# Convolution groups 1 to 3 of a two-layer hybrid block: weight columns stream past stationary tokens

## The chip, the cores and the metric

The kernel runs on one core of a Trainium2 chip. The metric is the device time of one execution in microseconds. Three executions before the change took 2537.07, 2537.81 and 2538.84 us; the median is 2537.81 us.

## The reference, cut to what matters

Two hybrid layers (a latent attention, pooling and convolution mixer), then a third block with attention and two wide feed-forward parts, on 256 tokens of width 2048. The change touches the convolution branch of both hybrid layers:

```python
D_CONV = 512; CONV_WIDTH = 3; DEPTH = 2

def conv_mixer(h, b_gate, c_gate, conv_w):
    u = c_gate * h
    y = lax.conv_general_dilated(u, conv_w[:, None, :], window_strides=(1,),
                                 padding=((CONV_WIDTH - 1, 0),), dimension_numbers=('NWC', 'WIO', 'NWC'),
                                 feature_group_count=D_CONV)
    return b_gate * y

def hybrid_layer(x, ...):
    proj = x @ w_in
    (q_lat, kv_lat, k_rope, g_mla, p_in, g_pool, c_h, c_b, c_c, g_conv) = jnp.split(proj, split_idx, axis=-1)
    y_mla = mla_mixer(...) * jax.nn.silu(g_mla)
    y_pool = pool_mixer(p_in, w_pool, pool_scale) * jax.nn.silu(g_pool)
    y_conv = conv_mixer(c_h, c_b, c_c, conv_w) * jax.nn.silu(g_conv)
    mix = jnp.concatenate([y_mla, y_pool, y_conv], axis=-1)
    out = mix @ w_out + b_out
    return layernorm(DEEPNORM_ALPHA * x + out, ln_g, ln_b)
```

## The kernel before, in words

All weights stream from HBM in slabs of up to 128 x 2048 numbers (1 MB), in one fixed order, written down by `plan()` as regions with so many slabs each. SyncE (SP) loads a slab into one of four `raw` buffers. ScalarE (ACT) rounds it to `high` (`split_high`, L1328), VectorE (DVE) makes `low = raw - high` (`split_low`, L1735), each in two halves of 1024 columns, into one of two buffers. The matrix engine (PE) multiplies high by high, high by low and low by high, so that fp32r matmuls give nearly fp32 results. Each engine's program goes through the same slots, one per slab (`walk`, L551). In a slot k, ACT makes the second half of slab k+1, then the steps of the slot, then the first half of slab k+2, then what it has to do with the finished products; DVE follows the same pattern. What else is done in a slot, attention heads among it, is given by the table `STEPS` (`layer_steps`, L224). Everything on an engine is in program order; other engines are waited for by semaphores.

There are two kinds of product. In a "tile" slab the weights are stationary: one slab is one tile of 128 output features by 256 tokens, and PE does 16 pairs, L923 with 512 moving columns (tokens high and low) and L927 with 256. In the regions `out`, `mem`, `heads`, `up` and `wide` the tokens are stationary and 512 weight columns stream past them: `product_natural` (L934) does three matmuls of 512 columns (L937 to L939) for each token block and each row of the slab, 24 per slab. The output then has tokens on the partitions.

Each hybrid layer has the regions `in_a`, `uq`, `uk`, `uv`, `in_b`, `in_c`, `pool`, `in_d`, `out`, `mem`. `in_d` has 13 tile slabs: the convolution's fourth tile of group 0, then four tiles (gate, h, c, b) for each of the groups 1 to 3. Six of the twelve are in `TURNED_OVER` (L342): eight L923 first and then eight L927, and so on. The other six alternate and have attention steps in their middle (`middle_of`, L941). For each tile, ACT copies the low half of the sum out of PSUM (L1382) and DVE adds the two halves (L1859, L1864). When a group is there, DVE multiplies h by c (L2087), applies the three taps (L2088 to L2091), multiplies by the silu of the gate (L2094) and by b (L1861) into `mix`. `mix` is split in four chunks of four tiles into `mixs`, high by ACT (L1684) and low by DVE (L2162). PE waits for chunk n of the order `MIX_ORDER` (L221; here 2, 0, 1, 3) at the start of slab n of `out` (L1164, semaphore `mix_l`). Chunk 3 is the convolution; its split was made between `in_d` and `out` (L1689, L2334).

The region `up` already turns token-major results back with DVE's 32 x 32 transposes (`hidden_turn`, L1778), and `wide` does so as well (L2007 to L2015). These are the forms that the change uses again.

Of the kernel before, what the change touches and what calls it, by code (L numbers as in the profile page):

```python
# [15 lines left out]
P = 128  # L16
# [64 lines left out]
def plan():  # L81
    regions = []
    for layer in range(DEPTH):
# [5 lines left out]
            Region(f"in_d{layer}", 13, (8, 8), 13, 2),  # L89
# [11 lines left out]
    s = t = g = pairs = lows = units = ups = wides = 0  # L101
    used = {}
    for r in regions:
# [6 lines left out]
        r.up, r.wide = r.name[:2] == "up", r.name[:4] == "wide"  # L110
# [4 lines left out]
        r.kind = next((k for n, k in (("up", "unit"), ("wide", "unit"), ("down", "down"), ("uq", "uq"), ("uk", "uk"), ("uv", "uv"),  # L115
# [5 lines left out]
        r.array = {"in_": "w_in", "uq": "w_uq", "uk": "w_uk", "uv": "w_uv", "pool": "w_pool", "out": "w_out",  # L121
# [3 lines left out]
                       next(n for n in ("in_", "uq", "uk", "uv", "pool", "out", "mem", "nat", "heads",  # L125
# [7 lines left out]
        r.span = 4 if r.up else WIDE  # L133
        r.unit0, r.up0, r.wide0 = units, ups, wides
        ups, wides = ups + r.up * r.n // r.span, wides + r.wide * r.n // r.span
        units = ups + wides
# [87 lines left out]
def layer_steps(layer):  # L224
    steps = {}

    def put(slot, *step):
        for name, first in (("in_a", 0), ("uq", 16), ("uk", 20), ("uv", 21), ("in_b", 23), ("in_c", 31),
                            ("pool", 33), ("in_d", 34), ("out", 48)):
# [31 lines left out]
    put(48 + 4, "shift", ln)  # L261
    put(48 + 5, "moments", ln, 0)
    put(48 + 8, "moments", ln, 1)
    put(48 + 12, "moments", ln, 2)
    for n in range(4):
        put(48 + 10 + n, "memory", 8 * layer + 2 * n, 8 * layer + 2 * n + 2)
# [94 lines left out]
def build(nc, t):  # L361

    with ExitStack() as ctx:
# [18 lines left out]
        memk = at("memk", [P, MEM, S], F32)  # L382
        memv = at("memv", [P, TB, MEM * P], F32)
# [50 lines left out]
        stage = at("stage", [P, TB, 2 * S], F32)  # L434
        scale_b = at("scale_b", [P, 2 * S], F32)
# [71 lines left out]
        unit_scaled = sem("unit_scaled")  # L507
        wide_out, wide_turned, wide_added, wide_squared, wide_folded = (
# [88 lines left out]
        def unit_bank(r, k, b):  # L597

            n = r.unit_in_part + k // r.span + int(r.name[-2])
# [226 lines left out]
        def acc_of(r, T):  # L826
# [3 lines left out]
            if r.name == "mixout" and T < r.t0 + 2 or after_norm(r) and r.t0 + 2 <= T < r.t0 + 4 \  # L830
                    or r.name == "down11" and T < r.t0 + 2:
                return flat(score[T % 2][:, :, :])
            return acc[T % 2][:, :]
# [12 lines left out]
        def gates_done(layer, tile):  # L846

            return 10 * layer + (tile // 4 + 1 if tile < 8 else tile - 5)
# [71 lines left out]
        def _(eng):  # L920
# [20 lines left out]
            def middle_of(r, k):  # L941
# [5 lines left out]
                if r.name[:4] == "in_d":  # L947
                    return (8, 9, 10, 11, 11 + 2 * r.layer, 12 + 2 * r.layer, 8)[k // 2]
                return 8

            def slot(r, k, i):
# [3 lines left out]
                halfway = [x for x in steps if r.kind in ("tile", "natural") and (  # L955
                    r.kind == "tile" and x[0] in ("turn", "mixv", "lat_sum") or x not in SCORES_FIRST and x[0] in ("memory_feature", "scores", "forget_turn", "cum", "decay")
# [11 lines left out]
                def bank_free(tile, per):  # L968
# [68 lines left out]
                elif r.kind == "unit":  # L1037
                    u, q_ = divmod(k, r.span)
                    if q_ == 0:
# [8 lines left out]
                    last_row = KT - 1 if r.up else CT - 1  # L1048
                    for piece in range(2):
                        piece_ready(piece)  # L1050
                        for b in range(TB):
                            for c in range(per):
                                row = 4 * q_ + per * piece + c
# [4 lines left out]
                                last = product_natural(unit_bank(r, k, b), (xs if r.up else hidden)[:, row, :],  # L1058
# [112 lines left out]
            def unit_bank_free(r, u, i):  # L1171
# [7 lines left out]
                else:  # L1179
                    eng.wait_ge(stored, val(r.t0 + 4 * (u - 1), 4, i))  # L1180

# [145 lines left out]
        def _(eng):  # L1327
# [13 lines left out]
            def slot(r, k, i):  # L1341
# [44 lines left out]
                if last_of_unit(r, k):  # L1386
                    (unit_gates if r.up else wide_copies)(r, k + 1 - r.span, i)
# [18 lines left out]
            def wide_copies(r, k, i):  # L1406
# [4 lines left out]
                for b in range(TB):  # L1411
# [4 lines left out]
                    eng.activation(wide_nat[:, b, :], unit_bank(r, k, b), ACT.Copy, scale=0.5).then_inc(wide_out, 1)  # L1416

# [313 lines left out]
        def _(eng):  # L1731
# [66 lines left out]
            def store(r, k, i, tile, per):  # L1798
# [19 lines left out]
                if r.name[:3] == "out":  # L1818
                    b, w = tile % TB, slice(512 * (tile // TB), 512 * (tile // TB + 1))
                    done(eng.tensor_tensor(z[:, b, w], acc[T % 2][:, :], x_tok[:, b, w], ALU.add))  # L1820
# [36 lines left out]
                elif r.name[:4] == "in_d" and tile % 4 == 0:  # L1857

                    done(eng.tensor_tensor(branch[:, 2, :], first, second, ALU.add), True)  # L1859
                    g = (tile + 3) // 4  # L1860
                    ins = eng.tensor_tensor(mix[:, 12 + g, :], mix[:, 12 + g, :], branch[:, 2, :], ALU.mult)  # L1861
                    final(ins, r.layer + 1 if g == GROUPS - 1 else None)
# [3 lines left out]
            def final(ins, count):  # L1866

                if count:
                    ins.then_inc(mix_final, 1)
                    eng.wait_ge(mix_final, count)  # L1870
                else:
                    step_(ins)
# [622 lines left out]
```

## Time and profile before

| what | value |
|---|---|
| median of three executions | 2537.81 us (2537.07 to 2538.84) |
| the profiled execution, its own time | 2537.32 us |
| its span, first to last instruction | 2535.5 us |
| PE busy | 2513.9 us, 99% |
| DVE busy | 1848.0 us, 73% |
| ACT busy | 1315.6 us, 52% |
| HBM read | 475.72 MB, 188 GB/s over the span |
| granted TensorE clock, mean | 1.000 |

PE's busy time is the union of its matmuls; they are pipelined, so the pitch from start to start says what one costs, not its duration. The DMA share is that of the core's 16 DMA engines. The chain of work that ended last lies on PE for 83% of the span.

### The profile page before, as it was taken

What the parts mean: (1) busy time and instruction counts of PE and PEld (TensorE: products, weight loads), DVE (VectorE), ACT (ScalarE), POOL (GpSimd) and SP (SyncE); (2) the same over time, 40 slices, a digit from 0 to 9 for tenths busy, and PEclk for the clock granted to TensorE, in tenths of its full rate; (3) what the DMA queues carried; (4) which work ended last, traced back from release to release, by engine and by line L of the source; (5) the groups of instructions that cost most, each with busy time, mean ns of one, the idle gap of its engine ahead of it and who ended that gap; (6) DMA issues with size and microseconds to landing.
All of it is one profiled execution on the core that took longest, in us unless ns stands there. A gap on an engine that the chain in (4) does not pass through costs nothing.

```text
span 2535.5 us, 33176 instructions
## 1 busy us (share of the span) xinstructions
PE 2513.9 (99%) x12124; PEld 2111.3 (83%) x12124; DVE 1848.0 (73%) x2980; ACT 1315.6 (52%) x1893; POOL 17.5 (1%) x20
## 2 busy tenths in 40 slices
PE   7999999999999999999999999999999999999999
PEld 6888888888888888888888887888888888888888
DVE  8777658777658777677777785678777767777766
ACT  6665565565566444444444454775544444444443
POOL 2000000000000000000000000000000000000000
PEclk9999999999999999999999999999999999999999
DMA  7554556454555555555555554444555555555554
GB/s 302 200 187 176 193 189 232 169 192 170 198 184 191 191 198 190 192 184 204 193 199 178 185 201 149 150 151 171 194 196 187 197 183 199 199 193 190 198 183 150
DMA packets 71519, 480.84 MB, mean 190 GB/s; under 512 B 8032, under 2 KB 10720, under 8 KB 18144
## 3 DMA queue, kind: packets, MB, share of 16 engines
q1 hardware_dynamic: 71392, 479.16, 53.5%
q8 instruction: 78, 1.28, 0.2%
q14 instruction: 49, 0.40, 0.0%
HBM read 475.72 MB, written 2.10 MB: 188 GB/s over the span
## 4 chain that ended last, share of the span: by engine, by line
PE 83%; DVE 1%; ACT 1%; issue 0%; ACTq 0%; DVEq 0%
PE acc L937 13%; PE acc L939 12%; PE acc L938 12%; PE score L937 9%; PE score L938 9%; PE score L939 9%; PE acc L923 9%; PE acc L927 4%; PE score L923 1%; PE score L1263 1%; PE score L927 1%; PE head_ps L1286 0%; DVE low L1740 0%; PE turn_ps L1272 0%; PE head_ps L1287 0%
## 5 line engine op out<-in xcount | busy, mean ns | idle before, releaser
L1740 DVE TENSOR_TENSOR low<-raw,high 128x1024 fp32r<-128x1024 f32 (+3 forms) x916 | 1080.2, 1184 | 473.2 <-ACT high L1338 464.7
L1338 ACT ACTIVATE high<-raw 128x1024 fp32r<-128x1024 f32 (+3 forms) x916 | 935.6, 1024 | 848.9 <-PE acc L939 447.6
L923 PE MATMUL acc<-xs,high 128*128 128x512 f32 x1184 | 396.4, 397 | 2.5 <-DVE xs L2275 2.2
L937 PE MATMUL acc<-high,xs 128*128 128x512 f32 x960 | 379.4, 395 | 2.3 <-DVE v_nat L1833 1.9
L939 PE MATMUL acc<-low,xs 128*128 128x512 f32 x960 | 374.1, 390 | 0.0
L938 PE MATMUL acc<-high,xs 128*128 128x512 f32 x960 | 373.6, 389 | 0.0
L927 PE MATMUL acc<-xs,low 128*128 128x256 f32 x1184 | 298.0, 279 | 0.0
L937 PE MATMUL score<-high,xs 128*128 128x512 f32 x704 | 274.0, 389 | 0.0
L939 PE MATMUL score<-low,xs 128*128 128x512 f32 x704 | 273.9, 389 | 0.0
L938 PE MATMUL score<-high,xs 128*128 128x512 f32 x704 | 273.9, 389 | 0.0
L923 PEld LDWEIGHTS acc<-xs,high 128*128 128x128 f32 x1184 | 219.4, 188 | 50.7 <-DVE xs L2275 3.1
L1787 DVE STREAM_TRANSPOSE unit_turn<-unit_prod 32x128 f32<-32x128 f32 x704 | 212.9, 302 | 9.8
L927 PEld LDWEIGHTS acc<-xs,low 128*128 128x128 f32 x1184 | 212.0, 188 | 4.2
L937 PEld LDWEIGHTS acc<-high,xs 128*128 128x128 f32 x960 | 180.2, 188 | 41.9 <-issue 4.6
L939 PEld LDWEIGHTS acc<-low,xs 128*128 128x128 f32 x960 | 180.2, 188 | 38.2
L938 PEld LDWEIGHTS acc<-high,xs 128*128 128x128 f32 x960 | 180.3, 188 | 36.5
L939 PEld LDWEIGHTS score<-low,xs 128*128 128x128 f32 x704 | 132.1, 188 | 27.5
L937 PEld LDWEIGHTS score<-high,xs 128*128 128x128 f32 x704 | 132.1, 188 | 27.4
L938 PEld LDWEIGHTS score<-high,xs 128*128 128x128 f32 x704 | 132.1, 188 | 27.4
L937 PE MATMUL score<-high,hidden 128*128 128x512 f32 x308 | 119.8, 389 | 0.0
L938 PE MATMUL score<-high,hidden 128*128 128x512 f32 x308 | 119.8, 389 | 0.0
L939 PE MATMUL score<-low,hidden 128*128 128x512 f32 x308 | 119.8, 389 | 0.0
(399 smaller groups left out, 3222.5 us busy)
## 6 DMA issues: line engine op xcount, KB each, us to landing
raw<-w_up_dram SPq DMA_DIRECT2D x176, 1024.0 KB, 4.8
raw<-w_in_dram SPq DMA_DIRECT2D x76, 1024.0 KB, 4.9
raw<-w_wide_dram SPq DMA_DIRECT2D x70, 1024.0 KB, 4.8
raw<-w_out_dram SPq DMA_DIRECT2D x32, 1024.0 KB, 4.8
raw<-w_heads_dram SPq DMA_DIRECT2D x24, 1024.0 KB, 4.8
raw<-w_mixout_dram SPq DMA_DIRECT2D x16, 1024.0 KB, 4.8
raw<-w_down_dram SPq DMA_DIRECT2D x16, 704.0 KB, 4.0
raw<-w_mem_dram SPq DMA_DIRECT2D x8, 1024.0 KB, 4.7
```

Source lines behind the costliest of these rows:

```text
L923: return eng.matmul(bank_, hi, moving, start=start, stop=False)
L927: return eng.matmul(bank_[:, 0:S], lo, moving[:, 0:S], start=False, stop=stop)
L937: eng.matmul(bank_, xh, hi, start=start, stop=False)
L938: eng.matmul(bank_, xl, hi, start=False, stop=False)
L939: return eng.matmul(bank_, xh, lo, start=False, stop=stop)
L1263: last = eng.matmul(score[n % 2][:, b, 0:w], qc[:, b * P:(b + 1) * P], kc[:, 0:w], start=(m == 0), stop=(m == len(qk) - 1))
L1338: eng.activation(high[:, s % SPLIT, to:to + n * P], raw[:, s % RAW, at_:at_ + n * P], ACT.Copy).then_inc((highs_a, highs_b)[piece], 1)
L1740: eng.tensor_tensor(low[:, s % SPLIT, w], raw[:, s % RAW, at_:at_ + n * P], high[:, s % SPLIT, w].bitcast(F32), ALU.subtract).then_inc((lo ...
L1787: ins = eng.transpose(to[QUAD * j:QUAD * (j + 1), n, :, :, :], from_[QUAD * n:QUAD * (n + 1), j, :, :, :])
```

## The change

`in_d` keeps one slab. Groups 1 to 3 become a new region `conv` of twelve slabs, three units of four, laid out in `w_in` by rows: each unit has 2048 x 512 weights, the four tiles of a group side by side. PE computes a unit with tokens stationary, into one bank for each of the two token blocks. The banks come from `acc0`, `acc1` and `sums`. At a unit's end ACT copies both banks to `conv_nat` (512 columns, tokens on partitions) and takes the silu of the gate columns in place. DVE multiplies h by c and silu(g) by b in that layout (`conv_gate`), turns the two products into `branch` with 16 transposes (`conv_move`, in two halves), applies the taps and multiplies once (`conv`). These steps stand in slots 4, 5 and 6 after the unit's first slab; for group 3 that is in slots 0, 1 and 2 of `out`. The split of chunk 3 moves from between the regions to slot 2 of `out`. The second tile of `out` is computed in `sums`.

```diff
-            Region(f"in_d{layer}", 13, (8, 8), 13, 2),
+            Region(f"in_d{layer}", 1, (8, 8), 1, 2), Region(f"conv{layer}", 4 * (GROUPS - 1), (8, 8), 0, 2),
...
-        put(33 + 4 * g, "silu", layer, 12 + g, 13 + g)
-        put(34 + 4 * g, "conv", layer, g)
+        if g:
+            put(35 + 4 * g, "conv_gate", layer, g)
+            put(35 + 4 * g, "conv_move", layer, g, 0)
+            put(36 + 4 * g, "conv_move", layer, g, 1)
+            put(37 + 4 * g, "conv", layer, g)
+        else:
+            put(33, "silu", layer, 12, 13)
+            put(34, "conv", layer, 0)
     for slot, c in zip((44, 45), MIX_ORDER[layer]):
         put(slot, "mix_split", layer, c)
+    put(49, "mix_split", layer, MIX_ORDER[layer][3])
...
-    TURNED_OVER |= {(f"in_d{_l}", k) for k in (1, 3, 5, 7, 9, 11)}
...
         def unit_bank(r, k, b):
+            if r.conv:
+                a, c = (acc[(r.t0 + n) % 2][:, :] for n in range(2))
+                return ((a, sums[:, :]), (c, a), (sums[:, :], c))[k // r.span][b]
...
+                    elif r.name[:3] == "out" and tile < 4:
+
+                        if tile == 2:
+                            eng.wait_ge(stored, r.t0 + 1)
+                        eng.wait_ge(conv_out, 2 * REG[f"conv{r.layer}"].conv0 + (4, 5, 5, 6)[tile])
...
                         for b in range(TB):
+                            if r.conv and q_ == 0 and piece == 0:
+                                conv_bank_free(r, u, b)
                             for c in range(per):
+                                if r.conv and 4 * piece + 2 * b + c == (middle + 1) // 2:
+                                    for step in halfway:
+                                        do(*step)
...
+            def conv_bank_free(r, u, b):
+
+                if u == 0:
+                    eng.wait_ge(stored, REG[f"in_d{r.layer}"].t0)
+                elif u == 1 and b == 0:
+                    eng.wait_ge(stored, REG[f"in_d{r.layer}"].t0 + 1)
+                else:
+                    eng.wait_ge(conv_out, 2 * r.conv0 + {(1, 1): 1, (2, 0): 2, (2, 1): 3}[u, b])
...
+            def conv_copies(r, k, i):
+
+                n = r.conv0 + k // r.span
+                if n:
+                    eng.wait_ge(conv_gated, n)
+                for b in range(TB):
+                    if b == 0:
+                        eng.wait_ge(unit_half, halves_till(r, k, i))
+                    else:
+                        eng.wait_ge(products, r.g0 + 2 * (k + r.span))
+                    eng.activation(conv_nat[:, b, :], unit_bank(r, k, b), ACT.Copy).then_inc(conv_out, 1)
+                eng.wait_ge(conv_out, 2 * n + 2)
+                eng.activation(conv_nat[:, :, 0:P], conv_nat[:, :, 0:P], ACT.Silu).then_inc(conv_silu, 1)
...
-                    for c in MIX_ORDER[n][2:]:
+                    for c in MIX_ORDER[n][2:3]:
                         do("mix_split", n, c)
...
+                elif kind == "conv_gate":
+                    layer, g = a
+                    n = REG[f"conv{layer}"].conv0 + g
+                    eng.wait_ge(conv_silu, n)
+                    eng.tensor_tensor(conv_prod[:, :, P:S], conv_nat[:, :, P:2 * P], conv_nat[:, :, 2 * P:3 * P], ALU.mult)
+                    eng.tensor_tensor(conv_prod[:, :, 0:P], conv_nat[:, :, 0:P], conv_nat[:, :, 3 * P:4 * P], ALU.mult)\
+                        .then_inc(conv_gated, 1)
+                    eng.wait_ge(conv_gated, n)
+                elif kind == "conv_move":
+                    layer, g, half = a
+                    from_ = conv_prod[:, :, :].rearrange("p b (m j f) -> p j b m f", m=2, f=QUAD)
+                    to = branch[:, 0:2, :].rearrange("p m (b q s) -> p q b m s", b=TB, s=QUAD)
+                    for n in (2 * half, 2 * half + 1):
+                        for j in range(P // QUAD):
+                            ins = eng.transpose(to[QUAD * j:QUAD * (j + 1), n, :, :, :], from_[QUAD * n:QUAD * (n + 1), j, :, :, :])
+                    if half:
+                        ins.then_inc(conv_turned, 1)
                 elif kind == "conv":
...
+                    if g:
+                        eng.wait_ge(conv_turned, REG[f"conv{layer}"].conv0 + g)
+                        u = branch[:, 1, :]
...
+                    if g:
+                        ins = eng.tensor_tensor(mix[:, 12 + g, :], branch[:, 0, :], y, ALU.mult)
...
+                    if g == GROUPS - 1:
+                        ins.then_inc(mix_final, 1)
+                        eng.wait_ge(mix_final, layer + 1)
```

On DVE, at the border from `in_d` to `out` in a layer, the rows before are these (`mixs` are the splits, `low` the low parts of weight slabs; the two rows with `mix<-mix` end group 3):

```order
L2088 TENSOR_SCALAR scale_c<-silu_g,par 128x256
L2090 SCALAR_TENSOR_TENSOR scale_c<-silu_g,par,scale_c 128x255
L2090 SCALAR_TENSOR_TENSOR scale_c<-silu_g,par,scale_c 128x254
L2094 TENSOR_TENSOR mix<-mix,scale_c 128x256
L1740 TENSOR_TENSOR low<-raw,high 128x1024
L1859 TENSOR_TENSOR branch<-acc,lowsum 128x256
L1861 TENSOR_TENSOR mix<-mix,branch 128x256
L2162 TENSOR_TENSOR mixs<-mix,mixs 128x4x256 x2
L1740 TENSOR_TENSOR low<-raw,high 128x1024 x7
L1820 TENSOR_TENSOR z<-acc,x_tok 128x512 x2
```

In the changed kernel DVE has, after the split of chunk 1 (`mixs`), up to the first result of `out` (`z`):

```order
L1787 TENSOR_TENSOR low<-raw,high 128x1024
L2120 TENSOR_TENSOR conv_prod<-conv_nat 128x2x128
L2121 TENSOR_TENSOR conv_prod<-conv_nat 128x2x128
L2130 STREAM_TRANSPOSE branch<-conv_prod 32x2x2x32 x8
L1787 TENSOR_TENSOR low<-raw,high 128x1024 x2
L2130 STREAM_TRANSPOSE branch<-conv_prod 32x2x2x32 x8
L1787 TENSOR_TENSOR low<-raw,high 128x1024 x2
L2147 TENSOR_SCALAR scale_c<-branch,par 128x256
L2149 SCALAR_TENSOR_TENSOR scale_c<-branch,par,scale_c 128x255
L2149 SCALAR_TENSOR_TENSOR scale_c<-branch,par,scale_c 128x254
L2153 TENSOR_TENSOR mix<-branch,scale_c 128x256
L2229 TENSOR_TENSOR mixs<-mix,mixs 128x4x256
```

The split of chunk 3, the last row, has moved behind five low parts and all of group 3's work. On ACT, at the same border, the rows before were:

```order
L1382 ACTIVATE lowsum<-acc 128x256
L1338 ACTIVATE high<-raw 128x1024 x2
L1382 ACTIVATE lowsum<-acc 128x256
L1684 ACTIVATE mixs<-mix 128x4x256 x2
L1338 ACTIVATE high<-raw 128x1024 x9
```

They are now:

```order
L1461 ACTIVATE conv_nat<-sums 128x512
L1461 ACTIVATE conv_nat<-acc 128x512
L1463 ACTIVATE conv_nat<-conv_nat 128x2x128
L1731 ACTIVATE mixs<-mix 128x4x256
L1371 ACTIVATE high<-raw 128x1024 x5
L1731 ACTIVATE mixs<-mix 128x4x256
L1371 ACTIVATE high<-raw 128x1024 x4
```

The two copies and the silu of group 3 stand in front of the split of chunk 1, and the split of chunk 3 stands five high parts later.

## Rows read from the trace of the kernel before

**Rows 1.** The page: busy time of each engine.

```profile
PE 2513.9 (99%) x12124; PEld 2111.3 (83%) x12124; DVE 1848.0 (73%) x2980; ACT 1315.6 (52%) x1893; POOL 17.5 (1%) x20
```

**Rows 2.** PE's waits, longest first: total us, times, longest.

```profile
PE score L1314 <- DVE z L2235: 13.1, 1, 13.1
PE acc L923 <- DVE xs L2275: 2.2, 3, 1.0
```

**Rows 3.** Windows on PE: stretch, length, busy (count), clock, DMA share, GB/s.

```profile
213.32:288.07 74.75, 74.75 (x438) 1.00 0.49 171
276.94:282.52 5.58, 5.58 (x34) 1.00 0.40 135
282.53:288.07 5.54, 5.54 (x34) 1.00 0.54 191
298.98:304.42 5.44, 5.44 (x26) 1.00 0.56 200
258.58:265.12 6.54, 6.54 (x41) 1.00 0.53 210
1668.38:1674.85 6.47, 6.47 (x33) 1.00 0.28 91
```

**Rows 4.** Window on DVE over `in_d` of layer 0, same columns.

```profile
207.00:288.00 81.00, 58.85 (x101) 1.00 0.50 174
```

**Rows 5.** Timeline of DVE: start us, us, instruction.

```profile
211.22 0.42 DVE L2087 TENSOR_TENSOR silu_g<-branch 128x256 f32<-128x256 f32 x1
211.67 0.35 DVE L2088 TENSOR_SCALAR scale_c<-silu_g,par 128x256 f32<-128x256 f32 x1
...
213.10 0.42 DVE L2094 TENSOR_TENSOR mix<-mix,scale_c 128x256 f32<-128x256 f32 x1
...
300.33 1.23 DVE L1740 TENSOR_TENSOR low<-raw,high 128x1024 fp32r<-128x1024 f32 x1 [1.50 <-ACT high L1338]
...
999.57 1.23 DVE L1740 TENSOR_TENSOR low<-raw,high 128x1024 fp32r<-128x1024 f32 x1 [0.39 <-ACT high L1338]
1000.71 2.50 DVE L1787 STREAM_TRANSPOSE unit_turn<-unit_prod 32x128 f32<-32x128 f32 x8
1003.23 1.23 DVE L1740 TENSOR_TENSOR low<-raw,high 128x1024 fp32r<-128x1024 f32 x1
```

**Rows 6.** Timeline of ACT, same columns.

```profile
256.72 0.42 ACT L1621 ACTIVATE mix<-mix 128x256 f32<-128x256 f32 x1
257.05 1.04 ACT L1338 ACTIVATE high<-raw 128x1024 fp32r<-128x1024 f32 x1
...
263.57 0.38 ACT L1667 ACTIVATE turned<-turn_ps 128x256 f32<-128x256 f32 x1 [3.46 <-PE turn_ps L1272]
...
264.01 1.06 ACT L1338 ACTIVATE high<-raw 128x1024 fp32r<-128x1024 f32 x1
...
299.24 1.06 ACT L1338 ACTIVATE high<-raw 128x1024 fp32r<-128x1024 f32 x1 [1.66 <-PE acc L939]
```

**Rows 7.** Groups of instructions by form: count, busy us, mean ns, idle before.

```profile
L1787 DVE STREAM_TRANSPOSE unit_turn<-unit_prod 32x128 f32<-32x128 f32 x704 | 212.9, 302 | 9.8
L2013 DVE STREAM_TRANSPOSE wide_turn<-wide_nat 32x256 f32<-32x256 f32 x224 | 97.6, 436 | 3.6
L1416 ACT ACTIVATE wide_nat<-score 128x512 f32<-128x512 f32 x14 | 7.5, 584 | 0.0
```

**Rows 8.** Timeline of DVE and PE around a wait in `nat0`.

```profile
1529.44 0.48 DVE L1833 TENSOR_SCALAR v_nat<-acc,token 128x256 f32<-128x256 f32 x1 [1.27 <-ACT v_nat L1434]
...
1530.07 0.47 PE L937 MATMUL acc<-high,xs 128*128 128x512 f32 x1 [1.94 <-DVE v_nat L1833]
```

**Rows 9.** Timeline of PE: the attention steps in slab 8 of `in_d`.

```profile
262.39 0.59 PE L1286 MATMUL head_ps<-turned,v_mla 128*128 128x256 f32 x2
```

**Rows 10.** Timeline of PE at the launch.

```profile
13.14 1.94 PE L1314 MATMUL score<-par,z 128*128 128x128 f32 x8 [13.14 <-DVE z L2235]
...
20.40 1.03 PE L1314 MATMUL score<-par,z 128*128 128x128 f32 x8
```

More of the change, by code:

```diff
@@ L100, in plan @@
                 regions.append(Region(f"down{part}{c}", 2 * tail, (6, 5), tail, 2))
-    s = t = g = pairs = lows = units = ups = wides = 0
+    s = t = g = pairs = lows = units = ups = wides = convs = start = 0
     used = {}
@@ L114, in plan @@
         r.per = 2 if r.name[:3] == "mem" else 4
-        r.kind = next((k for n, k in (("up", "unit"), ("wide", "unit"), ("down", "down"), ("uq", "uq"), ("uk", "uk"), ("uv", "uv"),
+        r.kind = next((k for n, k in (("up", "unit"), ("wide", "unit"), ("conv", "unit"), ("down", "down"), ("uq", "uq"), ("uk", "uk"), ("uv", "uv"),
                                       ("pool", "pool"), ("mem", "natural"), ("nat", "natural"), ("heads", "natural"),
@@ L124, in plan @@
                    "down2": "w_down2"}[
-                       next(n for n in ("in_", "uq", "uk", "uv", "pool", "out", "mem", "nat", "heads",
+                       next(n for n in ("in_", "conv", "uq", "uk", "uv", "pool", "out", "mem", "nat", "heads",
                                         "mixout", "up1", "up2", "wide1", "wide2", "down1", "down2") if r.name.startswith(n))]
@@ L132, in plan @@
             r.loop = (4, 8, 4)
[L133 to L136, printed above, removed]
+        r.span = WIDE if r.wide else 4
+        r.unit0, r.up0, r.wide0, r.conv0 = units, ups, wides, convs
+        ups, wides, convs = (n + kind * r.n // r.span for n, kind in ((ups, r.up), (wides, r.wide), (convs, r.conv)))
+        units = ups + wides + convs
         if r.name in ("up10", "up20"):
@@ L507, in build @@
         unit_scaled = sem("unit_scaled")
+        conv_out, conv_silu, conv_gated, conv_turned = (sem(n) for n in ("conv_out", "conv_silu", "conv_gated", "conv_turned"))
         wide_out, wide_turned, wide_added, wide_squared, wide_folded = (
@@ L832, in acc_of @@
                 return flat(score[T % 2][:, :, :])
+            if r.name[:3] == "out" and T == r.t0 + 1:
+                return sums[:, :]
             return acc[T % 2][:, :]
@@ L954, in slot @@
                 middle = middle_of(r, k)
-                halfway = [x for x in steps if r.kind in ("tile", "natural") and (
-                    r.kind == "tile" and x[0] in ("turn", "mixv", "lat_sum") or x not in SCORES_FIRST and x[0] in ("memory_feature", "scores", "forget_turn", "cum", "decay")
+                halfway = [x for x in steps if (r.kind in ("tile", "natural") or r.conv) and (
+                    r.kind != "natural" and x[0] in ("turn", "mixv", "lat_sum") or x not in SCORES_FIRST and x[0] in ("memory_feature", "scores", "forget_turn", "cum", "decay")
                     or x[0] == "feature" and x[2] == 0)]
@@ L1038, in slot @@
                     u, q_ = divmod(k, r.span)
-                    if q_ == 0:
+                    if q_ == 0 and not r.conv:
                         unit_bank_free(r, u, i)
@@ L1057, in slot @@
                                 w = slice(at_, at_ + 512)
-                                last = product_natural(unit_bank(r, k, b), (xs if r.up else hidden)[:, row, :],
+                                last = product_natural(unit_bank(r, k, b), (hidden if r.wide else xs)[:, row, :],
                                                        high[:, pos_, w], low[:, pos_, w], b, row == 0, row == last_row)
@@ L1386, in slot @@
                 if last_of_unit(r, k):
-                    (unit_gates if r.up else wide_copies)(r, k + 1 - r.span, i)
+                    (unit_gates if r.up else wide_copies if r.wide else conv_copies)(r, k + 1 - r.span, i)
             def unit_gates(r, k, i):
@@ L1856, in store @@
                     done(ins, True)
-                elif r.name[:4] == "in_d" and tile % 4 == 0:
+                elif r.name[:4] == "in_d":
                     done(eng.tensor_tensor(branch[:, 2, :], first, second, ALU.add), True)
-                    g = (tile + 3) // 4
-                    ins = eng.tensor_tensor(mix[:, 12 + g, :], mix[:, 12 + g, :], branch[:, 2, :], ALU.mult)
-                    final(ins, r.layer + 1 if g == GROUPS - 1 else None)
+                    step_(eng.tensor_tensor(mix[:, 12, :], mix[:, 12, :], branch[:, 2, :], ALU.mult))
                 else:
                     done(eng.tensor_tensor(tile_dest(r, tile), first, second, ALU.add))
[L1866 to L1872, printed above, removed]
             def added(name, ins, last):
@@ L2407, in layout @@
     columns = np.concatenate(first + convs[:1] + pools + convs[1:])
-    out["w_in"] = np.concatenate([_tiles(a["w_in"][l], columns) for l in range(DEPTH)])
+    in_tiles = len(columns) // P - 4 * (GROUPS - 1)
+    out["w_in"] = np.concatenate([w for l in range(DEPTH) for w in (
+        _tiles(a["w_in"][l], columns[:in_tiles * P]), _rows(a["w_in"][l][:, columns[in_tiles * P:]], 4, 512))])
     per = P + ROPE
```

45 lines of the change are left out of this document (26 added, 19 removed).

## The prediction

> **What bounds the kernel now.** I read the page's totals first: the matrix engine (PE) is busy 99% of the span, VectorE (DVE) 73%, ScalarE (ACT) 52% [rows 1]. So I asked where PE waits. Its list of waits is nearly empty: 13.1 us at the launch, then nothing over 2.2 us in total [rows 2]. In the stretch that the change rewrites, twelve slabs of 1 MB in each layer, PE is busy 74.75 of 74.75 us in layer 0 [rows 3], and layer 1 repeats it. The time here is therefore the sum of PE's pitches, and the change can win only there. DVE is busy 58.85 of 81.00 us in the same place [rows 4]: it has some room, and the change puts new work on it. Loads are not what PE waits for: the DMA share in these windows is about half [rows 3, 4]. Two questions are left: how much shorter is a slab, and does the added DVE work reach PE.
>
> **Term 1, the pitch.** A slab in the old layout is 16 pairs, one matmul of 512 columns and one of 256; with tokens stationary it is 24 matmuls of 512. Both stream 12,288 columns. Without other steps in it the old slab takes 5.58 us (order turned over, six of the twelve) or 5.54 us (alternating, the other six); the new kind, as the output projection has it already, takes 5.44 us [rows 3]. Twelve slabs go from 6 x 5.58 + 6 x 5.54 = 66.72 us to 65.28 us: 1.44 us less per layer. The attention steps between the products stay, in five of the slabs. A group of them costs 6.54 - 5.54 = 1.00 us in an old slab and 6.47 - 5.44 = 1.03 us, for the same matmuls, in a slab of the new kind [rows 3]. I charge 0.02 us for each of the five: 1.34 us less per layer, 2.7 us in both.
>
> A rule of the Trainium skill would take this gain away. Its page "TensorE: Matmul & The Clock Gate" (Part 1, "Wait — 56ns, not 53.3ns?") gives start-to-start as columns over 2.4 GHz plus about 2.5 ns per matmul; by it an old slab is 5.20 us and a new one 5.18 us, 0.5 us in all. The measured slabs, 5.54 or 5.58 against 5.44 us, do not agree with it [rows 3].
>
> **Term 2, the last convolution group.** Before, the last group's gate and taps stood in front of the output projection, and DVE made both last splits of `mixs` back to back in its first slab. Now group 3 is copied out, gated, turned and filtered while the output projection runs, and its split stands in slot 2 of `out`. PE needs that split (`mix_l`) at the start of slab 3 of `out`. Call the start of `out` T; slab 3 would start at T + 3 x 5.44 = T + 16.32.
>
> - ACT: a slab's end reaches it 0.26 us after the next slab's start (window start 298.98, high part 299.24) [rows 3, 6]. Then the last copy, 0.58 us like `wide_nat` [rows 7], 0.02 to hand over, the silu 0.33 to the next start, and the split of chunk 1, 1.06 like a high part of the same size [rows 6]: T + 2.25. DVE starts 0.03 to 0.04 later (299.24 + 1.06 to 300.33) [rows 5, 6]: T + 2.29.
> - DVE then has a queue without a gap, in the order listed in the section on the change: split of chunk 1, 1.14 (like a low part, 999.57 to 1000.71); a low part, 1.14; two gate products, 0.42 + 0.45; eight transposes, 2.52; two lows, 2.28; eight transposes, 2.52; two lows, 2.28; taps, 1.43; the last product, 0.42 [rows 5]. Sum 14.60: T + 16.89. None of these lows waits: the last high part is ready at 2 x 5.44 + 0.26 + 1.06 = T + 12.2, and DVE comes to it at T + 13.9.
> - ACT's half of the split, 0.04 + 1.06; DVE's half, 0.04 + 1.23; PE follows 0.15 us after DVE's end (1529.44 + 0.48 to 1530.07), and its first matmul then takes 0.47 instead of 0.39 us [rows 8]. PE is back at T + 19.49.
>
> So PE stands for 19.49 - 16.32 = 3.17 us in each layer, 6.3 us in both. Everything on PE is queued behind this wait, and it is not won back: PE has no idle time later in which to lose it.
>
> **Term 3, the banks.** Unit 2's second token block uses the bank that unit 1's first copy frees (`conv_out`). ACT gets to that copy behind `turned` and a high part. In layer 1 the attention steps of that slab come after seven of its eight groups, at 4.76 us; `turned` starts 1.18 us after the first step (262.39 to 263.57), the high part 0.44 later [rows 6, 9]; the high part takes about 1.0 and the copy 0.58: 7.96 us, and 0.15 on to PE. PE wants the bank at 5.44 + 1.03 + 1.36 = 7.83 us. About 0.2 us, in layer 1 only; in layer 0 the steps come one group (0.68 us) earlier and nothing waits.
>
> **What costs nothing.** Per layer DVE loses 12 additions and 6 products of 0.42 us and gains 6 products and 48 transposes of 302 ns [rows 7], about 9 us more in a stretch in which it idles 22. PE covers that as long as each low part is ready for its slab; a low is made one to two slabs ahead, so a delay of some us is absorbed. I charge nothing before T, and up to 0.5 us per layer in the upper bound. ACT loses 12 `lowsum` copies and 3 silus and gains 6 copies and 3 silus. Bytes, DMA issues and their order are the same.
>
> **Sum.** -2.7 + 6.3 + 0.2 = +3.8 us. The profiled execution took 2537.32 us (span 2535.5), so such an execution would take 2541.1; it lies 0.5 under the median 2537.81, which gives 2541.6 us, 0.15% slower. About 0.2% (5.1 us, so 2532.7 to 2542.9) is what a measurement of this kernel can tell from no change.
>
> Bounds. Term 1: from 12 x (5.54 - 5.44) less five times 0.03, 1.05 us per layer, up to 12 x (5.58 - 5.44) = 1.68 us. Term 2: a transpose of 128 elements took 302 ns, one of 256 elements 436 ns [rows 7]; sixteen are in the queue, so 0 to 2.1 us more per layer. I take the form with the same element count. Below, the queue shrinks by 0.5 us if the products overlap with what follows. That the wait itself brings a gain is excluded: nothing on PE can pass it.
>
> **Rivals.**
> - The wait does not bind. DVE's 22 us of idle time speak for it; against it, the queue from T + 2.29 has no gap in which idle time could be used. -2.7 + 0.2: 2535.3 us. Chance 0.07.
> - Slower, by dearer transposes: they write 32-element pieces into `branch` and could cost what the wide ones do. 32 x 0.134 = 4.3 us more: 2545.9 us. It decides once the queues are 1.3 us longer than my sum, 40 ns for each transpose, that is from 342 ns. Against it: 704 of the same shape took 302 ns. Chance 0.07.
> - Slower, by the clock. At the launch, after 13.1 us without work, eight transposes on PE took 1.94 us where eight took 1.03 later [rows 10], and sixteen went at that pace: about 1.8 us lost. If a wait of 3 us sets this off, each layer loses 1.8 more: 2545.2 us. Against it: after PE's idle 1.94 us before 1530.07 no matmul doubled, the first took 0.47 us [rows 8]. But 3 us is more than any gap inside the run. Chance 0.08.
> - The pitch goes by columns alone: -0.5 + 6.5, 2543.8 us, just slower. Against it stand the measured slabs. Chance 0.04. The rule of the Trainium skill quoted above leads to this number.
>
> My forecast holds the other 0.74, with a range of its own of 2539.8 to 2543.4. Faster by over 0.2% needs more than any term offers: 0.03. Within 0.2%: most of the forecast and the first rival, 0.75. Slower by over 0.2%: the other three rivals and a tail of the forecast, 0.22. The range 2538.6 to 2545.2 leaves out the first rival and half of the dearer ones.
>
> **What the changed kernel's profile would show.** Term 1: `conv` slabs of 5.44 us where no attention step stands in them, and twelve slabs in 73.4 us instead of 74.7. Term 2: among PE's waits a row for `acc` released by the DVE split of `mixs`, twice, some 3 us each; DVE without idle time from the split of chunk 1 to the last convolution product. Term 3: one wait of 0.1 to 0.3 us for ACT's `conv_nat` copy. I am wrong if PE shows no such wait at slab 3 of `out`, if a `conv` slab takes 5.5 us or more, or if PE waits for low parts within `conv`, which would mean that DVE falls behind before T.

## The result

The changed kernel takes 2544.65 us (median of 13 runs, 2543.27 to 2546.2), the kernel before 2537.55 us (13 runs, 2537.07 to 2539.19). The ratio is 1.0026, 95% interval 1.0019 to 1.0034: 7.1 us or 0.28% slower. The forecast was 2541.6 us. The time lies in the range of 2538.6 to 2545.2, but 3 us above the forecast and outside the likeliest case's own range (2539.8 to 2543.4). It is slower by over 0.2%, to which I had given 0.22.

The profiled execution took 2545.82 us (span 2544.0), 8.5 us more than that of the kernel before. The page's first row, against [rows 1], shows that TensorE (PE) became busy for 4 us more, with 192 matmuls fewer:

```profile
PE 2517.9 (99%) x11932; PEld 2107.0 (83%) x11932; DVE 1865.7 (73%) x3052; ACT 1315.7 (52%) x1881; POOL 17.3 (1%) x20
```

PE's waits in the changed kernel (total us, times, longest), against [rows 2]:

```profile
PE score L1347 <- DVE z L2302: 13.2, 1, 13.2
PE acc L951 <- DVE mixs L2229: 6.0, 2, 3.0
PE acc L951 <- DVE v_nat L1880: 1.9, 1, 1.9
```

The second row is new: the wait for the split of chunk 3, once in each layer. The third is not; it is the wait in `nat0` of [rows 8]. Windows over single slabs of the changed kernel (length, busy of each engine, the granted clock, DMA share, GB/s), against [rows 3]:

```profile
225.93:231.38 5.45, 5.45 (x26) 4.50 (x24) 3.60 (x6) 3.00 (x6) 0.00 (x0) 1.00 0.32 96
281.26:286.70 5.44, 5.44 (x26) 4.50 (x24) 5.30 (x9) 2.72 (x3) 0.00 (x0) 1.00 0.59 197
...
297.58:306.16 8.58, 5.60 (x26) 4.35 (x24) 7.18 (x14) 3.59 (x4) 0.00 (x0) 0.94 0.68 244
306.16:314.42 8.26, 8.26 (x25) 6.57 (x26) 2.81 (x3) 1.48 (x2) 0.00 (x0) 0.65 0.35 127
314.42:319.86 5.44, 5.44 (x26) 4.50 (x25) 4.26 (x5) 3.35 (x6) 0.00 (x0) 1.00 0.65 197
...
681.74:690.32 8.58, 5.60 (x26) 4.35 (x24) 7.18 (x14) 3.59 (x4) 0.00 (x0) 1.00 0.70 244
690.32:697.45 7.13, 7.13 (x25) 5.73 (x25) 2.82 (x3) 1.48 (x2) 0.00 (x0) 0.76 0.38 147
```

The first two are `conv` slabs without an attention step: 5.45 and 5.44 us, as forecast. The third runs from the start of slab 2 of `out` to the start of slab 3, 8.58 us for 5.44 us of work: 3.14 us of lost time (PE's row gives 2.98 us of it as idle; the rest is the end of its last matmul, which the pitch leaves out). The fourth is slab 3 itself. It waits for nothing and takes 8.26 us instead of 5.44, with the granted clock at 0.65 on average. Layer 1 shows the same pair, 8.58 and 7.13. The slab after it is clean again. PE's timeline shows the cause inside slab 3:

```profile
302.79 0.39 PE L953 MATMUL sums<-low,mixs 128*128 128x512 f32 x1
306.16 0.77 PE L951 MATMUL acc<-high,mixs 128*128 128x512 f32 x1 [2.98 <-DVE mixs L2229]
306.72 0.63 PE L952 MATMUL acc<-high,mixs 128*128 128x512 f32 x1
307.15 0.63 PE L953 MATMUL acc<-low,mixs 128*128 128x512 f32 x1
```

From 306.72 the matmuls start 0.43 us apart, where 0.227 is the pitch elsewhere (24 in 5.44 us). That is the lower of the two clock levels, 1.2 instead of 2.4 GHz. Worked out from the windows' clock, it held for some 6.8 us in layer 0 (2 x 0.06 x 8.58 in the window of the wait, 2 x 0.35 x 8.26 in the slab) and for 3.4 us in layer 1.

The account for the profiled execution, read slab by slab: `in_d` and `conv` -1.40 and -1.38 us, a bank wait in layer 1 +0.29, two waits of 3.14, +6.3, and two slabs at a reduced clock, +2.82 and +1.69. The sum is 8.3 of the 8.5 us. Three of the four terms are the forecast's. The fourth, 4.5 us, is the rival that I gave 0.08. This execution is one of the three slowest of the 13 (granted clock 0.998 over the whole run, 0.999 in the ten from 2543.27 to 2544.83), so the median run lost less to the clock than this one.

### The profile page after: what moved, and what is told of

Read it like the earlier page. It is cut to its first block, busy times and chain, and to the rows that moved or that the text cites. A ratio compares the mean times of both kernels' runs of the same rounds, so it can differ in the third digit from the quotient of the medians.

```text
span 2544.0 us, 32809 instructions
## 1 busy us (share of the span) xinstructions
PE 2517.9 (99%) x11932; PEld 2107.0 (83%) x11932; DVE 1865.7 (73%) x3052; ACT 1315.7 (52%) x1881; POOL 17.3 (1%) x20
## 4 chain that ended last, share of the span: by engine, by line
PE 82%; DVE 1%; ACT 1%; issue 0%; ACTq 0%; DVEq 0%
PE acc L951 13%; PE acc L953 13%; PE acc L952 13%; PE score L951 9%; PE score L953 9%; PE score L952 9%; PE acc L937 7%; PE acc L941 4%; PE score L937 1%; PE score L1296 1%; DVE low L1787 1%; PE score L941 1%; PE head_ps L1319 0%; PE sums L951 0%; PE sums L953 0%; PE sums L952 0%
## 5 line engine op out<-in xcount | busy, mean ns | idle before, releaser
L951 PE MATMUL acc<-high,xs 128*128 128x512 f32 x1088 | 430.9, 396 | 2.3 <-DVE v_nat L1880 1.9
L953 PE MATMUL acc<-low,xs 128*128 128x512 f32 x1088 | 424.0, 390 | 0.0
L952 PE MATMUL acc<-high,xs 128*128 128x512 f32 x1088 | 423.5, 389 | 0.0
L937 PE MATMUL acc<-xs,high 128*128 128x512 f32 x800 | 274.4, 399 | 0.9 <-DVE xs L2342 0.7
L951 PEld LDWEIGHTS acc<-high,xs 128*128 128x128 f32 x1088 | 204.3, 188 | 47.1 <-issue 4.6
L953 PEld LDWEIGHTS acc<-low,xs 128*128 128x128 f32 x1088 | 204.2, 188 | 43.3
L952 PEld LDWEIGHTS acc<-high,xs 128*128 128x128 f32 x1088 | 204.4, 188 | 41.2
L941 PE MATMUL acc<-xs,low 128*128 128x256 f32 x800 | 209.2, 280 | 0.0
L937 PEld LDWEIGHTS acc<-xs,high 128*128 128x128 f32 x800 | 149.9, 189 | 34.8 <-DVE xs L2342 1.2
L941 PEld LDWEIGHTS acc<-xs,low 128*128 128x128 f32 x800 | 146.7, 190 | 2.0
```

What stands on the lines that cost most here:

```text
L937: return eng.matmul(bank_, hi, moving, start=start, stop=False)
L941: return eng.matmul(bank_[:, 0:S], lo, moving[:, 0:S], start=False, stop=stop)
L951: eng.matmul(bank_, xh, hi, start=start, stop=False)
L952: eng.matmul(bank_, xl, hi, start=False, stop=False)
L953: return eng.matmul(bank_, xh, lo, start=False, stop=stop)
```

## Experiments

My theory after the result: the wait of 3.1 us per layer costs itself and, behind it, a stretch at half clock, because PE stood still. Rivals: the half clock comes from the new natural slabs or the transposes; or another wait hides behind this one.

**The wait taken away.** DVE takes group 3's gate and first move before the split of chunk 1, and both engines take the split of chunk 3 at the head of slot 2. No byte, product or transpose is left out:

```diff
-        if g:
+        if g == GROUPS - 1:
+            put(48, "conv_move", layer, g, 1)
+            put(48, "conv", layer, g)
+        elif g:
             put(35 + 4 * g, "conv_gate", layer, g)
...
-    put(49, "mix_split", layer, MIX_ORDER[layer][3])
...
+                if r.name[:3] == "out" and k == 2:
+                    do("mix_split", r.layer, MIX_ORDER[r.layer][3])
...
+                    do("conv_gate", n, GROUPS - 1)
+                    do("conv_move", n, GROUPS - 1, 0)
```

> The changed kernel with one thing reordered on VectorE and ScalarE: group 3's gate, product, first and second move and taps are started before the split of chunk 1 instead of after it, and the split of chunk 3 stands at the head of slot 2 of `out`. The natural slabs, the transposes and every byte moved stay. Theory (the wait of 3.1 us a layer for `mix_l` of chunk 3 costs itself, and a stretch at half the granted clock after it costs the rest): both waits and both half-clock stretches are gone; -1.4 us a layer of pitch and +0.3 us of bank wait in layer 1 remain: 2537.55 - 2.8 + 0.3 = 2535.0 us, ratio to the kernel before 0.9990. Rival 1 (the half clock comes from the new natural slabs or the transposes, not from the wait): the waits go, the half clock stays, 2535.0 + 4.5 = 2539.5. Rival 2 (the work moved up makes another wait, at slab 1 or 2 of `out`): 2537 to 2541, with a new row of waits that names the line.

Measured: 2535.32 us (11 runs, 2535.0 to 2537.27), ratio 0.9990, interval 0.9981 to 0.9999. PE's waits hold no row for `mixs`. Windows of this kernel from slab 3 of `out`, in layer 0 (two slabs) and layer 1:

```profile
303.97:309.41 5.44, 5.44 (x26) 4.51 (x25) 3.65 (x5) 2.12 (x4) 0.00 (x0) 1.00 0.70 241
309.41:314.85 5.44, 5.44 (x26) 4.51 (x25) 4.18 (x5) 3.35 (x7) 0.00 (x0) 1.00 1.02 359
681.78:687.31 5.53, 5.53 (x25) 4.59 (x25) 3.95 (x4) 2.46 (x3) 0.00 (x0) 1.00 0.60 213
```

Wait and half clock are both gone from `out`. So neither the slabs nor the 96 transposes slow PE down, and DVE's 9 us per layer of additional work stay hidden. Its fastest runs lie 2.1 us under those of the kernel before beside it (2537.1); the theory had 2.5.

**The wait kept, PE busy in it.** The changed kernel, with matmuls into a scratch bank whose results nobody reads:

```diff
                     q_ = k % r.per
+                    if r.name[:3] == "out" and k == 3:
+                        for _ in range(13):
+                            eng.matmul(flat(turn_ps[:, :, :]), xs[:, 0, 0:P], xs[:, 0, :], start=True, stop=True)
```

> The changed kernel plus 13 matmuls of 512 columns into a scratch bank on TensorE just ahead of slab 3 of `out` in both layers: extra work without use, some 13 x 0.227 = 2.95 us, that lies inside the wait of 3.37 us. Theory (the clock falls because TensorE stood still for 3.4 us): slab 3 still starts where it did, at most 0.2 us later, but the granted clock stays full behind it and the 2.8 and 1.7 us of the two slow slabs are gone: 2544.65 - 4.5 = 2540.2 to 2541.4 us. Rival 1 (the clock falls for another reason, such as the load of all engines there): 2544.65 or a little more. Rival 2 (the extra matmuls delay what TensorE owes to others): up to 2 x 2.95 more, 2550.5.

Measured: 2541.84 us (11 runs, 2541.47 to 2544.42), ratio 1.0016, interval 1.0007 to 1.0026. Windows of this kernel over slab 3 of `out` with the 13 matmuls ahead of it (both layers), and over the slab after it in layer 0:

```profile
302.95:311.66 8.71, 8.67 (x39) 6.87 (x38) 4.72 (x6) 4.02 (x4) 0.00 (x0) 1.00 0.57 200
311.66:317.10 5.44, 5.44 (x26) 4.51 (x25) 4.26 (x5) 3.35 (x6) 0.00 (x0) 1.00 0.74 252
684.10:692.80 8.70, 8.67 (x39) 6.87 (x37) 4.72 (x6) 4.02 (x4) 0.00 (x0) 1.00 0.53 194
```

Slab 3 ends 3.27 us late, hardly more than the wait alone, and the clock stays full. Work without any use made the kernel 2.8 us faster than the changed kernel's median. The time is close to the forecast, 2541.6 us, which had this wait and no change of clock. It lies 0.4 us above the 2540.2 to 2541.4 that I had expected, for I had taken the 4.5 us that the profiled, slower execution lost off the median of all.

**The wait alone, without the change.** The kernel before, with the split of chunk 3 delayed on DVE:

```diff
+    put(50, "mix_split", layer, MIX_ORDER[layer][3])
...
-                    for c in MIX_ORDER[n][2:]:
+                    for c in MIX_ORDER[n][2:3]:
...
+                    for _ in range(13 if c == 3 and layer < DEPTH else 0):
+                        step_(eng.tensor_copy(scale_c[:, 0:S], branch[:, 0, :]))
```

> The kernel before, without any part of the change, given a wait of about the same length at the same place: the split of chunk 3 is put in slot 2 of `out`, with 13 copies of a 256-column tile on VectorE (about 0.33 us each, 4.3 us) ahead of its low part. TensorE then waits about 3 us for `mix_l` of chunk 3 in each layer. Theory: time of the kernel before + 2 x 3.1 + the half clock behind each wait (1.7 to 2.8 us each) = 2537.55 + 6.2 + 3.4 to 5.6 = 2547.1 to 2549.4 us, with granted clock 0.5 in the slab after each wait. Rival (a wait costs only its length; the half clock belongs to the changed work): 2543.8 us and full clock all through. If the copies fit in VectorE's slack: 2537.6.

Measured: 2544.79 us (8 runs, 2544.34 to 2546.82), ratio 1.0028. Its wait, and the windows over slab 2 with the wait (layer 0) and over slab 3 (both layers):

```profile
PE acc L938 <- DVE mixs L2165: 5.0, 2, 2.5
```

```profile
299.05:307.17 8.12, 5.60 (x25) 4.35 (x24) 6.33 (x16) 4.13 (x4) 0.00 (x0) 1.00 0.53 196
307.17:314.35 7.18, 7.18 (x25) 5.72 (x25) 2.82 (x3) 1.06 (x1) 0.00 (x0) 0.76 0.39 146
...
690.62:697.57 6.95, 6.95 (x24) 5.64 (x25) 2.82 (x3) 1.06 (x1) 0.00 (x0) 0.78 0.41 151
```

The waits came out shorter than I had planned, 2.68 us each (8.12 - 5.44) where I had said 3.1. That explains 0.8 of the 2.3 us by which the median lies under my 2547.1; the rest is that the clock cost less than I had charged, and in the median run less than in the profiled one (2545.85). The mechanism is the theory's: 5.4 us of wait, and 1.74 + 1.51 us of half clock in slabs that the change never touched. The waits alone would give 2543.0 us, and the fastest of the eight runs took 2544.34.

**How long a wait.** First longer, the same kernel with 26 copies:

> The kernel before with a made wait again, but 26 copies on VectorE in place of 13: 13 x 0.33 = 4.3 us more on top of the 2.69 us that 13 gave, so TensorE waits 7.0 us in each layer. Theory A (the half clock after a wait has a size of its own, 1.5 to 1.7 us lost, up to 2.8, whatever the wait's length): 2537.6 + 14.0 + 3 to 5.6 = 2554.6 to 2557.2. Theory B (the loss grows with the wait): over 2557.5. Theory C (the two are unrelated): 2551.6.

Measured: 2555.96 us (5 runs, 2555.41 to 2557.34), ratio 1.0070. Its waits, and the windows over slab 2 with the wait (layer 0) and over slab 3 (both layers):

```profile
PE acc L938 <- DVE mixs L2165: 13.6, 2, 6.8
```

```profile
299.04:311.44 12.40, 5.60 (x25) 4.34 (x24) 10.16 (x29) 4.13 (x4) 0.00 (x0) 0.81 0.35 129
311.44:319.61 8.17, 8.17 (x25) 6.50 (x25) 2.82 (x3) 1.06 (x1) 0.00 (x0) 0.66 0.35 128
...
700.13:708.53 8.40, 8.40 (x25) 6.64 (x26) 2.82 (x3) 1.06 (x1) 0.00 (x0) 0.64 0.36 125
```

The time lies in the range of theory A, and the loss does not follow the wait in proportion: the wait went up by 4.3 us, the loss behind it from 1.5 and 1.7 to 2.7 and 3.0 us. But it did grow, in both layers of the trace and in the times: the median less the waits (5.4 and 13.9 us) and the kernel before beside it leaves 1.8 us for the clock with 13 copies and 4.0 us with 26. So theory A's "whatever the wait's length" does not hold. Then shorter, the changed kernel with 4 and with 8 matmuls in the gap (`range(4)`, `range(8)` in the edit above):

> The changed kernel plus 4 matmuls of 512 columns without use ahead of slab 3 of `out` (0.9 us of the 3.37 us gap filled), which leaves TensorE idle for about 2.5 us per layer. Theory (the clock falls by the idle time, and 1.9 us in `nat0` was enough in some executions): it falls in most executions: 2541.8 + 1.7 to 3.4 = 2543.5 to 2545. Rival (only idle time of 3 us or more sets it off): 2541.8, as with 13 of them.

> The same with 8 matmuls (1.8 us filled, about 1.6 us idle per layer). Theory: less idle than in `nat0`, so the clock falls seldom or never at this place: median 2541.8 us, some runs up to 1.7 more. Rival (any idle time above a microsecond sets it off, or part of a slab's delay grows with it): 2543.5 to 2545.

Measured: 2543.38 us (11 runs, 2541.32 to 2544.74) with 4, and 2542.85 us (11 runs, 2541.41 to 2544.03) with 8. The wait and the windows over fillers and slab 3, with 4:

```profile
PE acc L951 <- DVE mixs L2232: 4.1, 2, 2.1
```

```profile
303.00:313.29 10.29, 8.22 (x29) 6.31 (x28) 4.73 (x6) 4.01 (x4) 0.00 (x0) 0.83 0.56 200
686.03:696.34 10.31, 8.23 (x29) 6.32 (x28) 4.74 (x6) 4.01 (x4) 0.00 (x0) 0.83 0.54 199
```

And with 8, where the last window is the one in `nat0`:

```profile
PE acc L951 <- DVE mixs L2232: 2.3, 2, 1.2
```

```profile
303.92:312.62 8.70, 7.54 (x34) 5.93 (x32) 4.72 (x6) 4.02 (x4) 0.00 (x0) 1.00 0.53 190
685.26:693.96 8.70, 7.53 (x33) 5.93 (x32) 4.73 (x6) 4.02 (x4) 0.00 (x0) 1.00 0.55 200
1530.00:1540.00 10.00, 8.05 (x32) 6.39 (x31) 4.65 (x10) 6.09 (x10) 0.00 (x0) 0.83 0.06 7
```

With 2.1 us of idle time the clock fell in both layers of the profiled execution (10.3 us where 8.7 stand without it), with 1.2 us in neither. The runs with 4 fillers spread from 2541.3 to 2544.7, so there the fall is not certain; two of the eleven, 2541.32 and 2541.59, have a granted clock of 1.000 over the whole run, the others 0.999. With 8 I had expected a median of 2541.8; it was 2542.85, and the trace shows where the profiled one lost its 1.6 us: in `nat0`. The other runs of that kernel have no trace, but each has its mean granted clock: 1.000 in the five up to 2542.14, 0.999 in the six from 2542.85. So the slower ones all had a fall; where it lay in them isn't known.

**The wait in `nat0`.** My evidence against the clock rival stood there [rows 8]. It is in all kernels, 1.9 us long, and the early order above lost 1.6 us behind it. So did the next kernel, the early order with one number more, on which the last experiments build:

```diff
-                    return (8, 9, 10, 11, 11 + 2 * r.layer, 12 + 2 * r.layer, 8)[(k + 1) // 2]
+                    return (8, 9, 10, 11, 11, 12 + 2 * r.layer, 8)[(k + 1) // 2]
```

The expectation calls the number a bank boundary. It is the place of the attention steps within a slab: in layer 1 they now come after six of the eight groups of products in place of seven, so that ACT gets to its copy earlier. No other bank is used, so the rival about one could not come.

> The kernel of the early order above (group 3's products ahead of the split of chunk 1) and one number more: the convolution's middle bank boundary is at 11 in both layers instead of 13 in layer 1, so that slab 9 of `conv` does not wait for the bank that `conv_out` frees. Theory: that wait, 0.31 us, is gone: 2534.7 us against 2535.0 for the early order alone. Rival (the bank that is used instead is itself still held): the same time or up to 1 us longer, with a wait on another bank.

Measured: 2536.31 us (11 runs, 2535.04 to 2537.42), ratio 0.9993, interval 0.9984 to 1.0002. The window over the ninth slab of `conv` (slab 8, as `out` is counted here) in layer 1 of the changed kernel, and then of this one:

```profile
648.10:653.85 5.75, 5.75 (x25) 4.43 (x24) 2.28 (x2) 5.58 (x8) 0.00 (x0) 1.00 0.39 162
```

```profile
642.04:647.50 5.46, 5.46 (x26) 4.51 (x24) 2.68 (x3) 4.88 (x7) 0.00 (x0) 1.00 0.43 176
```

The bank wait is gone, 0.29 us for the theory's 0.31, but the median is higher than without the edit, not lower, and the fastest runs of the two are alike (2535.04 and 2535.0): the times do not show the gain. Something of over a microsecond differs from run to run. PE's timeline of this kernel in `nat0` shows what it was in the profiled one:

```profile
1527.47 0.47 PE L953 MATMUL acc<-high,xs 128*128 128x512 f32 x1 [1.95 <-DVE v_nat L1886]
...
1528.72 0.63 PE L955 MATMUL acc<-low,xs 128*128 128x512 f32 x1
1529.14 0.63 PE L953 MATMUL acc<-high,xs 128*128 128x512 f32 x1
```

The clock fell after a wait of 1.95 us, the same wait after which [rows 8] shows none. Of the nine traces with this wait unfilled and unshortened, four show the fall (the early order, this one, and those with 13 and 8 matmuls) and five don't, the two kernels compared here among them. Two experiments test that this makes the runs differ. The gap was filled in this kernel and in the kernel before, with 8 matmuls into `head_ps[0]` where `r.name == "heads" and k == 0`:

> The early order with the bank boundary at 11 (the kernel run as e2), plus 8 matmuls of 512 columns without use (8 x 0.227 = 1.8 us) on TensorE just ahead of the first slab of `heads`, where every kernel of this study stands still for 1.9 us (`stored` of a `v_nat` tile). In the traces of the early orders a half-clock stretch followed that wait and cost 1.6 us; in those of the kernel before and the changed one none did. Theory (whether the clock falls there differs from execution to execution, and it falls only when TensorE has stood still): with the gap filled it never falls: all runs within 2534.9 to 2535.7 us, median 2535.1 against 2536.3 without the filling. Rival 1 (the spread of runs has another cause): the same spread, 2535.0 to 2537.4. Rival 2 (the filling delays the slab): up to 1 us more in every run.

> The kernel before, unchanged but for 8 matmuls of 512 columns without use (1.8 us) on TensorE ahead of the first slab of `heads`, inside its 1.9 us wait. The 27 runs of the kernel before beside the last experiments lie from 2536.8 to 2539.7. Theory (its upper runs are those in which the clock fell after the wait in `nat0`): all runs 2536.8 to 2538.0, none above 2538.4, median about 2537.3. Rival (the spread has another cause): the same spread up to 2539.7.

Measured: 2534.93 us (11 runs, 2534.56 to 2535.94), ratio 0.9987, interval 0.9978 to 0.9996; and 2537.66 us (11 runs, 2537.41 to 2538.26), ratio 0.9999, interval 0.9990 to 1.0008, with a median of 2538.05 (21 runs, 2536.94 to 2539.48) for the kernel before beside it. The upper runs are gone in both: the spread shrank from 2.4 to 1.4 us (a little wider than the 2534.9 to 2535.7 us of the expectation) and from 2.5 to 0.9 us. The medians moved by 1.4 and 0.4 us; the second is less than can be told from no change. The mean granted clock of each run says the same more sharply. Of the 21 runs of the kernel before, the 11 up to 2538.05 us have 1.000 and the 10 from 2538.66 us have 0.999; with the gap filled all 22 runs of the two kernels have 1.000.

**A version that beats both.** The gap in `nat0` can be shortened instead, since ACT had two activations ahead of the evacuation for which PE waits:

```diff
-STEPS.setdefault(("nat0", 3), []).append(("memory_key",))
+STEPS.setdefault(("heads", 0), []).append(("memory_key",))
```

> The early order with the bank boundary at 11, without any filling, and ScalarE's two `memory_key` activations (0.67 + 0.57 us) moved behind the evacuation of `nat0`'s last two tiles, which stands behind them in its queue. The tiles leave the bank 1.15 us earlier, so the gap of TensorE ahead of `heads` goes from 2.3 to about 1.2 us. Theory (the gap is set by ScalarE's queue, and the clock does not fall after a gap this short): 2534.93 (the filled version's median) - 1.15 = 2533.8 us, runs from 2533.4 to 2534.9, no half clock; below both kernels. Rival 1 (the table load ahead of the evacuation sets it, nothing gained): 2535 to 2536.3. Rival 2 (the later key delays the head steps that read it): over 2535.5, with a new wait.

Measured: 2533.69 us (11 runs, 2533.32 to 2534.0), ratio 0.9982, interval 0.9973 to 0.9991. The wait and the window behind it:

```profile
PE acc L953 <- DVE v_nat L1886: 0.8, 1, 0.8
```

```profile
1525.00:1535.00 10.00, 9.21 (x44) 6.91 (x43) 5.03 (x8) 5.97 (x9) 0.00 (x0) 1.00 0.29 105
```

It is 4.4 us faster than the kernel before beside it (2538.05) and has the narrowest spread of all, 0.7 us. The gain adds up: 2.8 us of pitch and 1.15 us of shorter wait make 3.9, and against those runs of the kernel before that have a granted clock of 1.000 (median 2537.36 us) it is 3.7; the rest is the fall of the clock, which half of the runs of the kernel before had and none of these has.

## Why the prediction was right and wrong

- **Term 1, the pitch, held.** -1.40 and -1.38 us for -1.34. The attention steps cost next to nothing more in the new slabs; I had charged 0.02 each. The rule of the Trainium skill weighed there (page "TensorE: Matmul & The Clock Gate", Part 1) led to an estimate of 0.5 us in all; the 2.8 us measured do not bear it out, and the rival built on pitch by columns alone falls with it.
- **Term 2, the last convolution group, held.** DVE's timeline in the changed kernel, with T at 286.70:

```profile
288.93 1.23 DVE L2229 TENSOR_TENSOR mixs<-mix,mixs 128x1024 fp32r<-128x1024 f32 x1 [1.03 <-ACT mixs L1731]
...
291.99 2.51 DVE L2130 STREAM_TRANSPOSE branch<-conv_prod 32x128 f32<-32x128 f32 x8
294.52 2.37 DVE L1787 TENSOR_TENSOR low<-raw,high 128x1024 fp32r<-128x1024 f32 x2
296.91 2.53 DVE L2130 STREAM_TRANSPOSE branch<-conv_prod 32x128 f32<-32x128 f32 x8
...
303.17 0.42 DVE L2153 TENSOR_TENSOR mix<-branch,scale_c 128x256 f32<-128x256 f32 x1
304.79 1.23 DVE L2229 TENSOR_TENSOR mixs<-mix,mixs 128x1024 fp32r<-128x1024 f32 x1 [1.19 <-ACT mixs L1731]
```

The queue starts at T + 2.23 (2.29 was said), has no gap, and ends at 303.59, T + 16.89. That this is the forecast's figure to the hundredth is luck: the queue began 0.06 us earlier and took 0.06 us longer. PE's next matmul starts at T + 19.46. The forecast had it start at T + 19.41, and its 19.49 held another 0.08 for a slower first matmul, so two small errors cancel in the 3.14 us for 3.17. The transposes took 303 ns each over 96, as their form in [rows 7], so the rival of dearer transposes falls, and so does the one in which the wait does not bind.
- **Term 3, the banks, had the right place.** One wait, in layer 1 only, of 0.29 instead of 0.2 us. The forecast's own terms, 7.96 + 0.15 - 7.83, add up to 0.28; it was rounded the wrong way.
- **"What costs nothing" held.** No wait for a low part before T; the early order shows it again.
- **The sum failed in one step: it charged nothing behind the wait.** After "PE is back" the sum counts slab 3 at its full pitch, 5.44 us; it took 8.26 and 7.13. The rival "slower, by the clock" was the right one. It named the mechanism, but took 1.8 us per layer from the launch [rows 10], where the traces have 1.5 to 3.0 us behind each wait of 2 us or more in `out`. The runs of the changed kernel, at 2544.65 in the middle, lie 3 us over the forecast: with 1.5 us per layer that is the whole miss, and the kernel with PE kept busy in its wait gave 2541.84. The measured time lies in the stated range only because the range ended at this rival's figure, 2545.2; the forecast's own mechanism does not reach it.
- **Why I gave it 0.08.** I took one execution as a rule. In [rows 8] the clock did not fall after 1.9 us of idle time, and I read this as evidence that it wouldn't; in four of nine traces it did. The three times that I had of the kernel before, 2537.07, 2537.81 and 2538.84 us, spread by as much as such a fall costs, and I did not ask why. And a row without a fall after 1.9 us says little of a wait that is half as long again. With the launch as the only row on a longer wait, and that one showing a loss, the rival deserved, as I judge it now, at least half of the chance, and the forecast would have been its 2545.2 us. The launch was weaker evidence than it looks, though: the profile gives a granted clock of 1.00 for the slow transposes there (13.14 to 16.81 us), so that the clock slowed them isn't shown. After the waits in `out` it reads 0.50.

## What to carry to other kernels

Where PE is the bound, charge a new wait of two or more microseconds inside the run with its length and, as these traces had it, 1.5 to 3 us more for the clock behind it. Over all runs it is less, since not every run pays in full: by the medians 0.9, 1.7 and 2.0 us for each wait of 2.7, 3.1 and 7.0 us. After the 1.9 us in `nat0`, 33 of the 78 runs of the kernel before beside the experiments have the lower mean clock. A layout that shortens PE's work is worth its gain only if its last producer is early: look at the order of the slower engine's queue first, since here a reordering turned +7.1 us into -2.3 us. And a spread between runs of one kernel is a reading too: compare it with what one rare event would cost before a row that shows no event is taken as proof.

## What the runs showed that I had not expected

- After a wait of PE, the granted clock was at half for some 3.4 us (waits of 1.9 to 2.5 us, where it fell at all), 3.4 and 6.8 us (waits of 3.0 us) and 10.3 us (waits of 6.8 us, by the clock of their windows). Part of such a stretch can lie within the wait, where it costs nothing.
- The same wait, with the same work around it, is followed by a fall in one execution and by none in the next: 1.9 us, four of nine traces. What decides it is open. After waits of 0.8 and 1.2 us no trace shows one.
- The fall does not come at a fixed point of the wait: in layer 0 of the changed kernel it began within it (granted clock 0.94 in the wait's window), in layer 1 only after PE had resumed (1.00 there, 0.76 in the next), and in `nat0` a microsecond after (1527.47 to 1528.72).
- Idle time can be filled with matmuls whose results are thrown away, and the kernel gets faster: by 2.8 us in `out`. The delay of slab 3 grew by 0.1 us per layer with them (3.27 us against 3.14).
